# Layer 1 of a two-layer trunk: one matmul for a head's sum of squares, and two more heads' keys turned by transfers

## The reference, cut to what matters

```
u = rmsnorm(h);  q, f_pre, i_in, gate = u @ w_in        # 2048 columns each, 16 heads of 128
f = lb + (1-lb) * sigmoid(f_pre);  k = 1 - f            # log f is summed up inside a chunk: b
o = masked(q e^b . k e^-b) v + (q e^b) state            # o: 512 positions x 128 features
state = e^b_last * state + (k e^(b_last-b))^T v
o = o * rsqrt(mean(o * o over the head's 128 features) + eps) * norm_g
y = (o * silu(gate)) @ w_out;  h = h + y
```

## Time and profile before

| | us |
|---|---|
| median of 3 runs | 1579.25 (1578.45 to 1579.79) |
| the profiled execution | 1578.75 |
| its span, first to last instruction | 1577.0 |
| PE busy in the span | 1569.5 |
| PEld, DVE, ACT, POOL busy | 1305.2, 813.1, 639.5, 399.6 |

### The profile page before, as it was taken

The page is one execution under the profiler, slowest core; times in us unless marked ns, Lnnn a source line. Parts: engine busy times, 40 slices in busy tenths (PEclk is TensorE's granted clock), DMA queues, the critical chain, the costliest instruction groups (busy, mean ns, idle before and its releaser), DMA issues.

```text
span 1577.0 us, 24101 instructions
## 1 busy us (share of the span) xinstructions
PE 1569.5 (100%) x8707; PEld 1305.2 (83%) x8707; DVE 813.1 (52%) x1439; ACT 639.5 (41%) x1114; POOL 399.6 (25%) x766
## 2 busy tenths in 40 slices
PE   9999999999999999999999999999999999999998
PEld 8888888888887888888888888888888888888887
DVE  7874685586577733544333454433245541434445
ACT  6563563464354543333232433332343342243333
POOL 5211011013300082222273211248022225502210
PEclk9999999999999999999999999999999999999999
DMA  6434223223621453444344444436344434534422
GB/s 190 114 88 121 83 87 110 84 87 110 187 80 43 123 148 94 118 106 90 114 136 119 113 100 97 105 94 164 85 117 117 110 74 132 143 91 112 107 77 67
DMA packets 278534, 171.04 MB, mean 108 GB/s; under 512 B 69248, under 2 KB 251216, under 8 KB 278448
## 3 DMA queue, kind: packets, MB, share of 16 engines
q1 hardware_dynamic: 212512, 139.64, 32.3%
q0 software_dynamic: 23792, 29.13, 6.0%
q10 hardware_dynamic: 42144, 1.05, 1.5%
HBM read 144.37 MB, written 5.71 MB: 95 GB/s over the span
## 4 chain that ended last, share of the span: by engine, by line
PE 95%; POOL 3%; DVE 1%; issue 0%; ACT 0%; DMA 0%; POOLq 0%; ACTq 0%
PE proj L571 82%; PE inner L571 3%; POOL v L525 2%; PE inner L953 2%; PE inner L948 2%; PE inner L884 1%; PE inner L820 1%; PE inner L906 1%; PE inner L823 1%; PE inner L784 1%; PE inner L809 1%; POOL v L534 0%; PE proj L717 0%; PE inner L898 0%; PE inner L830 0%
## 5 line engine op out<-in xcount | busy, mean ns | idle before, releaser
L1407 DVE TENSOR_TENSOR w_lo<-raw,w_hi 128x1024 fp32r<-128x1024 f32 x252 | 307.4, 1221 | 458.7 <-ACT w_hi L1001 455.6
L571 PE MATMUL proj<-u_hi,w_hi 128*128 128x512 f32 x1280 | 505.4, 395 | 0.0
L571 PE MATMUL proj<-u_hi,w_lo 128*128 128x512 f32 x1280 | 498.8, 390 | 0.0
L571 PE MATMUL proj<-u_lo,w_hi 128*128 128x512 f32 x1280 | 498.6, 390 | 0.0
L1001 ACT ACTIVATE w_hi<-raw 128x1024 fp32r<-128x1024 f32 x252 | 265.4, 1054 | 177.3 <-PE proj L571 116.4
L571 PEld LDWEIGHTS proj<-u_hi,w_lo 128*128 128x128 f32 x1280 | 240.3, 188 | 51.1
L571 PEld LDWEIGHTS proj<-u_hi,w_hi 128*128 128x128 f32 x1280 | 240.4, 188 | 49.7 <-ACT qk L1017 0.4
L571 PEld LDWEIGHTS proj<-u_lo,w_hi 128*128 128x128 f32 x1280 | 240.5, 188 | 48.1
L545 POOL DMA_DIRECT2D rows<-qx x240 | 118.0, 500 | 260.3 <-DVE qx L1835 258.5
L571 PE MATMUL proj<-w_hi,u_hi 128*128 128x512 f32 x440 | 173.7, 395 | 0.0
L571 PE MATMUL proj<-w_lo,u_hi 128*128 128x512 f32 x440 | 171.5, 390 | 0.0
(11 more groups left out here) (219 smaller groups left out, 1662.1 us busy)
## 6 DMA issues: line engine op xcount, KB each, us to landing
raw<-at_w_in SPq DMA_DIRECT2D x160, 512.0 KB, 4.3
raw<-hg_w_in SPq DMA_DIRECT2D x63, 512.0 KB, 4.0
rows<-qx POOLq DMA_DIRECT2D x240, 44.0 KB, 2.7
raw<-hg_w_out SPq DMA_DIRECT2D x16, 512.0 KB, 3.5
raw<-at_w_out SPq DMA_DIRECT2D x16, 512.0 KB, 4.7
v<-rows POOLq DMA_DIRECT2D x64, 64.0 KB, 2.0
v<-qk POOLq DMA_DIRECT2D x192, 16.0 KB, 3.3
v<-x SPq DMA_DIRECT2D x4, 512.0 KB, 6.4
```

Of the source, the lines that this page charges most:

```text
L571: ins = nc.tensor.matmul(bank[:, :], stationary(a), moving(b), start=(first and n == 0), stop=(last and n == 2))
L1407: nc.vector.tensor_tensor(w["lo"][:, slot, :], raw[:, slot, :], w["hi"][:, slot, :].bitcast(F32), ALU.subtract).then_inc(w_ready, 1)
```

## The change

Fourteen heads (all but the last two) are now of the kind `by_transfer`: the 12 of the loop, and heads 0 and 1 of the fourth quad, whose keys PE turned before. For these heads the squares are formed in two activations, features 0 to 63 and features 64 to 127, both on partitions 0 to 63; DVE adds the two, ACT copies the sum's high part to partitions 0 to 63, DVE writes the low part to partitions 64 to 127 of the same tile, and one matmul with ones sums all 128 rows. The norm sum moves from behind half 4 to behind the next head's scores, and for a quad's last head to behind half 5. `out_rstd` moves down to ahead of `sigmoid`, `y_high` and `y_low` into the next head's turn, and DVE's `gate` behind `mask_scores`. POOL's loop holds the moves of the next quad's first two heads at its end; its bias work comes behind the moves of the fourth quad's head 1.

```diff
+        LAST_TURNED = 2
+        def by_transfer(last, h):
+            return not last or h < LAST_TURNED
...
-            quads(pool, hg_body)
+            for h in range(LAST_TURNED):
+                move_keys(0, h)
+            with pool.Fori(0, NQ - 1) as q:
+                for h in range(LAST_TURNED, HQ):
+                    move_keys(q, h)
+                turn_chunks(q)
+                for h in range(LAST_TURNED):
+                    move_keys(q + 1, h)
...
                 pe.wait_ge(osq_ready, g + 1)
+                if transfer:
+                    nc.tensor.matmul(p_ss[:, :], ones_r[:, :], osq["hi"], start=True, stop=True).then_inc(osum_done, 1)
+                    return
...
-                elif half == 3 + late:
-                    norm_sum(g)
+                elif half == 3 and not transfer:
+                    norm_sum(g, transfer)
+                elif half == 5 and transfer and h == HQ - 1:
+                    norm_sum(g, transfer)
+                if half == 0 and h and by_transfer(last, h - 1):
+                    norm_sum(g - 1, True)
...
             def square(g, transfer):
                 act.wait_ge(O_done, g + 1)
+                if transfer:
+                    nc.scalar.activation(tmp[low_half, 0, :], p_O[low_half, :], ACT.Square)
+                    nc.scalar.activation(tmp[low_half, 1, :], p_O[high_half, :], ACT.Square).then_inc(squared, 1)
+                    act.wait_ge(halves_added, g + 1)
+                    nc.scalar.activation(osq_hi[low_half, :], tmp[low_half, 0, :], ACT.Copy).then_inc(osq_hi_ready, 1)
+                    return
...
@@ ACT, hg_body
+                    if h > 1 and by_transfer(last, h - 2):
+                        y_high(head(q, h - 2), h - 2)
...
                     split_hi(HG, q, 3 * h + Q_, last)
-                    if late:
-                        out_rstd(before)
...
-                    if late and h < HQ - 1:
-                        y_high(before, h - 1)
...
+                    if late:
+                        out_rstd(before)
                     sigmoid(g)
...
@@ DVE
+            def add_halves(g):
+                dve.wait_ge(squared, g + 1)
+                nc.vector.tensor_tensor(tmp[low_half, 0, :], tmp[low_half, 0, :], tmp[low_half, 1, :], ALU.add)\
+                    .then_inc(halves_added, 1)
...
+                    nc.vector.tensor_tensor(osq_hi[high_half, :], tmp[low_half, 0, :], osq_hi[low_half, :].bitcast(F32),
+                                            ALU.subtract).then_inc(osq_ready, 1)
...
-                    if h:
-                        osq_low(before, late)
+                    if late:
+                        add_halves(before)
...
                     decays(link, q, h, g, soon and h == HQ - 1, by_transfer(last, h))
+                    if late:
+                        osq_low(before, True)
                     split_lo(HG, q, 3 * h + Q_, last)
-                    if late and h < HQ - 1:
-                        hg_output(link, before)
...
                     split_lo(HG, q, 3 * h + G_, last)
-                    if late and h == HQ - 1:
+                    if late:
                         hg_output(link, before)
```

More of the change, by code:

```diff
@@ L173, in program @@
         osq = {"hi": osq_hi[:, :], "lo": osq_lo[:, :]}
+        low_half, high_half = slice(0, P // 2), slice(P // 2, P)
         rstd = sb("rstd", [P, S])
@@ L312, in own_keys @@
         def own_keys(g):
-            return g - (H - HQ) + 1
+            return g - (H - HQ + LAST_TURNED) + 1
         def quads(eng, body):
@@ L432, in body @@
                         h = (n - SLOTS) // HG.per_head
-                        if layer is HG and n - SLOTS == h * HG.per_head and 0 <= h < HQ and by_transfer(last):
+                        if layer is HG and n - SLOTS == h * HG.per_head and 0 <= h < HQ and by_transfer(last, h):
                             wait_turn(sp, sp_met, keys_turned, head(q, h) + 1)
@@ L825, in outputs, with norm_sum, recurrence @@
                 ins.then_inc(O_done, 1)
-            def norm_sum(g):
+            def norm_sum(g, transfer):
                 pe.wait_ge(osq_ready, g + 1)
+                if transfer:
+                    nc.tensor.matmul(p_ss[:, :], ones_r[:, :], osq["hi"], start=True, stop=True).then_inc(osum_done, 1)
+                    return
                 nc.tensor.matmul(p_ss[:, :], ones_r[:, :], osq["hi"], start=True, stop=False)
                 nc.tensor.matmul(p_ss[:, :], ones_r[:, :], osq["lo"], start=False, stop=True).then_inc(osum_done, 1)
-            def recurrence(g, h, half, transfer):
+            def recurrence(g, h, half, last):
+                transfer = by_transfer(last, h)
                 late = 1 if transfer else 0
@@ L849, in hg_body @@
                         if h:
-                            recurrence(head(q, h - 1), h - 1, half, by_transfer(last))
+                            recurrence(head(q, h - 1), h - 1, half, last)
                 for half in range(KT):
@@ L855, in hg_body @@
                         values(HG, q, 0, half // 2, half % 2)
-                    recurrence(head(q, HQ - 1), HQ - 1, half, by_transfer(last))
+                    recurrence(head(q, HQ - 1), HQ - 1, half, last)
                 out_projection(HG, q, last)
@@ L1168, in square @@
                 act.wait_ge(O_done, g + 1)
-                nc.scalar.activation(square_of(transfer), p_O[:, :], ACT.Square).then_inc(squared, 1)
+                if transfer:
[4 more added lines that the diff above has]
+                    return
+                nc.scalar.activation(enb[:, :], p_O[:, :], ACT.Square).then_inc(squared, 1)
                 act.wait_ge(squared, g + 1)
-                nc.scalar.activation(osq["hi"], square_of(transfer), ACT.Copy).then_inc(osq_hi_ready, 1)
+                nc.scalar.activation(osq["hi"], enb[:, :], ACT.Copy).then_inc(osq_hi_ready, 1)
             def out_rstd(g):
@@ L1192, in hg_body @@
                     g, before = head(q, h), head(q, h - 1) if h else None
-                    late, soon = h and by_transfer(last), h and not by_transfer(last)
+                    late, soon = h and by_transfer(last, h - 1), h and not by_transfer(last, h - 1)
                     number, bank, _ = HG.event(q, 3 * h + F_)
@@ L1224, in hg_body @@
                     split_hi(HG, q, 3 * h + G_, last)
-                    if by_transfer(last):
+                    if by_transfer(last, h):
                         keep_keys(g)
-                    if late and h < HQ - 1:
-                        y_high(before, h - 1)
-                    if h == HQ - 1 and not by_transfer(last):
+                    if h == HQ - 1 and not by_transfer(last, h):
                         kT_copy(g)
+                    if late:
+                        out_rstd(before)
                     sigmoid(g)
-                    if late and h == HQ - 1:
-                        y_high(before, h - 1)
                 g = head(q, HQ - 1)
-                square(g, by_transfer(last))
+                if by_transfer(last, HQ - 2):
+                    y_high(g - 1, HQ - 2)
+                square(g, by_transfer(last, HQ - 1))
                 if not last:
@@ L1704, in hg_body @@
                     g, before = head(q, h), head(q, h - 1) if h else None
-                    late, soon = h and by_transfer(last), h and not by_transfer(last)
+                    late, soon = h and by_transfer(last, h - 1), h and not by_transfer(last, h - 1)
                     if h:
+                        mask_scores(before)
+                        if h > 1 and by_transfer(last, h - 2):
+                            dve.wait_ge(y_made, head(q, h - 2) + 1)
                         gate(HG, q, h - 1, before, 3 * (h - 1) + G_)
-                        mask_scores(before)
                     wait_emptied(dve, HG, q, 3 * h + F_)
                     bound(ef, sigf_bounded)
+                    if h > 1 and by_transfer(last, h - 2):
+                        y_low(head(q, h - 2), h - 2)
                     if h:
@@ L1716, in hg_body @@
                     split_lo(HG, q, 3 * h + F_, last)
-                    if h:
-                        osq_low(before, late)
+                    if late:
+                        add_halves(before)
                     if soon:
+                        osq_low(before, False)
                         hg_output(link, before)
-                    decays(link, q, h, g, soon and h == HQ - 1, by_transfer(last))
+                    decays(link, q, h, g, soon and h == HQ - 1, by_transfer(last, h))
+                    if late:
+                        osq_low(before, True)
                     split_lo(HG, q, 3 * h + Q_, last)
-                    if late and h < HQ - 1:
-                        hg_output(link, before)
                     if soon and h < HQ - 1:
@@ L1729, in hg_body @@
                     split_lo(HG, q, 3 * h + G_, last)
-                    if late and h == HQ - 1:
+                    if late:
```

(14 more changed lines are left out.)

10 lines of the change are left out of this document (4 added, 6 removed).

## The result

The changed kernel takes 1581.06 us (median of 22 runs, 1580.4 to 1582.28), the kernel before 1578.88 in the same series (22 runs; one of them took 5193 us, the others 1578.21 to 1579.79). The ratio is 1.0015, 95% interval 1.0009 to 1.0021: slower by 2.2 us, which is small but real. The forecast was 0.3 us slower, within a range of 1575.3 to 1582.0. The sign, the class (no difference by the bound of 0.2%, which the interval's upper end just passes) and the range held. Of the 2.2 us the forecast had 0.3, and the missing 2 us are what the experiments look for. The profiled execution took 1581.47 us, its span 1579.8.

A forecast was written before the change was run, and what follows sets the result against it. PE's row of instructions was taken as the time, other engines counting only where PE waits. Terms -3.2 - 0.8 + 3.8 + 0.5 = +0.3 us gave 1579.0 profiled, 1579.5 median; range 1575.3 to 1582.0.

The forecast's parts named there:

- Part 1: Norm sums of 14 heads: one matmul fewer each at 0.227 us of PE, 3.2 us less.
- Part 2: Fourth quad, keys of two more heads by transfers: 0.42 us of PE saved each, 0.8 us less.
- Part 5: Fourth quad, head 1 to head 2: PE's updates wait for ACT's later key copy, 0.5 us more.
- Part 3: Loop quad's end: later norm sum delays output tile 0's split, PE waits at first column; 1.26 each, 3.8 us more.
- Part 4: Same chain inside a quad: osq_low is ready 0.6 to 0.8 us before PE's norm sum, so no cost.
- Part 6: POOL's bias work, moved later beside DVE's recurrence in the fourth quad: covered by 186 us, costs nothing.
- rival C: POOL's additions and DVE lock each other out in one stretch: 1581.8 us; chance 0.04.
- A: Rival: full gain of 4.0 us, neither the first-column nor the key-copy wait comes, 1575.2 us; chance 0.13.
- B: Rival: operations crossing partitions take longer, PE waits behind scores of 11 heads; 5.7 us at twice, 1585.2; chance 0.09.
- D: Rival: at the quad's end the single norm sum waits for its squares; 2 us to spare, given no chance.

The follow-up runs named there:

- e3_both: Changed kernel with both the first-column split moved earlier and the value-tile reordering (osq_low behind both splits): 1574.70 us, ratio 0.9976 to the kernel before.
- e7_double: Changed kernel with the single norm matmul of each of the 14 heads done twice: 1583.47 us, ratio 1.0031 to the kernel before.
- e1_column: Changed kernel with ACT's split of output tile 0 ahead of y_high, DVE's part behind hg_output, in loop quads' last heads: 1576.61 us, ratio 0.9988.
- e8_half4: Changed kernel with the norm sum of a loop quad's last head put back behind half 4: 1579.81 us, ratio 1.0006 to the kernel before.
- e2_value_tiles: Changed kernel, loop quads' last head: osq_low behind both splits, norm sum behind one half, mask_scores ahead of hg_output: 1578.70 us, ratio 1.0002.
- e4_key_copy: Changed kernel with ACT's copy of head 2's turned keys in the fourth quad put between out_rstd and sigmoid: 1580.30 us, ratio 1.0011.
- e9_both_again: Rerun of the changed kernel with the column-split and value-tile moves, in one series with e10_all_again: 1576.48 us, ratio 0.9982 to the kernel before.
- e10_all_again: Rerun of the changed kernel with the column-split, value-tile and key-copy moves, in one series with e9_both_again: 1575.90 us, ratio 0.9977.
- e6_keys_by_pe: Changed kernel with no head of the fourth quad turned by transfers, that quad as before, loop as changed: 1581.78 us, ratio 1.0020.
- e5_all: Changed kernel with all three moves (column's split, value tiles, key copy): 1574.95 us, ratio 0.9977 to the kernel before.

## Why the prediction was right in its sign and class, and 2 us short

**Part 1 (-3.2), right.** Each of three quads with nothing left to wait for takes 122.89 to 122.92, the old quad less four matmuls of 0.227 (e3_both), and doubling the matmul costs 0.227 wherever PE does not wait just behind it (e7_double).

**Part 2 (-0.8), right within what can be told.** The fourth quad gave 0.17 less than its terms say, and 0.1 of that is the slower updates behind the wait for the key copy, which belongs to part 5. The rest is open.

**Part 3 (+3.8), right.** 6.76 us from the norm matmul to the split against 6.83, 1.31 a quad by e1_column against 1.26, so 3.9. The squares were in time as worked out: PE waits for them only at half 4 (e8_half4), and there by less than 1 us.

**Part 4 ("so nothing"), the step that failed.** It followed `osq_low` from its new place forward to its own user, PE's norm sum, and found 0.6 to 0.8 us to spare. That holds nearly: in the turn of head 2 `osq_low` ends at 219.68 and PE's norm matmul starts at 220.23, 0.55 later, and PE never waits for it behind the scores. But `osq_low` was moved to ahead of DVE's next split, and the step did not ask who waits for that. In the turns of heads 1 and 2 PE never comes to wait for the split. In the turn of head 3 the next two splits are for value tiles 2 and 3, and the first is wanted right behind the scores, with 0.5 us to spare before. The rows for it were in the same stretch (at 239.26, is that very start). e2_value_tiles takes away these waits and leaves those at the column: 2.1 us between the medians, 0.6 in each quad's window. This term is 3 x 0.6 = 1.8, and with 0.15 of part 3 and 0.17 in the fourth quad it makes up the 2.1 between +0.3 and +2.4.

Part 3 had the rule and part 4 did not apply it: of a step that is moved, what is queued behind it counts, in each turn of the loop on its own. Head 3's turn differs from the others in what its splits feed.

**Part 5 (+0.5), right.** 0.49 in the trace and 0.1 more for the slower updates behind it; 0.4 in the fourth quad's window by e4_key_copy, which gives 0.2 back at the outputs; 0.6 between e9_both_again and e10_all_again.

**Part 6 (nothing), right, with something seen in it.** The row that it went by was thinner than it says, since the first of the three splits in the earlier trace rows, at 386.86, is over before the additions start. But DVE's operations beside POOL's additions do take what they take without them, and it is POOL that is stretched, from 10.07 to 14.54 us. e6_keys_by_pe, with POOL's work at its old place, is no faster for it. The Trainium skill (SBUF — State Buffer, section "SBUF: two separate sides") has the two lock each other out, and by it rival C gave DVE a loss. The trace agrees that the two engines hold each other up, with POOL's 4.5 us, and shows no loss of DVE.

**The rivals.** A (1575.2) was refuted for the change as it is, and is what e5_all and e10_all_again give once three rows of the order are changed: its mechanism, that the saving is PE's own and whole, is right. It was wrong only in leaving out the chains. B needs longer rows across partitions, and there are none: the squares 0.59 and 0.60, the addition 0.68, the subtraction 0.69, the figures of the full-width rows, and no PE wait for `osq_hi`. Half the partitions do not make them cheaper either. C is answered above. D did not come: the squares were ready at 255.03 and PE came at 257.02, 2.0 us later, as forecast.

So the change does what it says and gives 4.0 us, and the order of ACT's and DVE's work gives back 3.9 at the first columns, 1.8 at the value tiles and 0.5 at the key copy. None of these waits was needed. With all three moved, 1574.95 us (ratio 0.9977 to before), the change is faster than both kernels.

## What to carry to other kernels

When PE is never idle, each matmul less is worth its start-to-start time, and the change is decided by the chains on the engines around it. For every operation that is moved or put in, list what is queued behind it on its own in-order engine, up to the next idle gap, and for each of these the time at which its user comes for it; do this for each turn of the loop that differs, not for the typical one. The user may also come sooner, since the removed work moves PE's whole row forward: spare time is lost from both sides. And compare windows between the same landmarks, as the start of an execution can move by more than the effect.

## What the runs showed of the hardware

POOL's 28 small additions took 14.54 us beside DVE's operations of the fourth quad, and 10.07 at their old place; with the old place restored (e6_keys_by_pe) they took 10.07 again, and 14.56 in e3_both, which leaves them at the new one. DVE's rows beside them did not lengthen: `w_lo` took 1.20 us there and in the same place of quad 2 without them. At the old place too it was POOL that gave way: an addition of one column that starts at 397.22 took 1.32 us beside DVE's `w_lo` at 397.25 (1.23 us), where the first addition, of 12 columns, took 0.32 at 388.47. Why POOL's operations get longer there is not isolated by any run here.

An activation or a DVE operation on 64 partitions cost the same as on 128 (0.59 and 0.60 us for the square, 0.69 for the subtraction), also where the input's partitions were the upper ones and the output's the lower, or the other way round.
